# Gate matrix in DRAM: from blocks of sixteen columns per store to blocks of eight rows per load

## The chip, the cores and the metric

One core of a Trainium2 chip runs the whole program. The metric is the device time of one execution in microseconds, lower is better.

## The reference, cut to what matters

Two passes of one trunk layer (a context of 128 tokens and 1,024 latent tokens, nine tiles of 128 tokens in all) end in the PEER channel mixer. For every token, eight heads each choose 16 of 16,384 experts; the expert rows are dotted with the token, passed through gelu, weighted, and used to sum rows of a second table:

```
s = jnp.einsum('thpd,hpkd->thpk', q, keys)
v1, i1 = lax.top_k(s[:, :, 0], PEER_TOPK)
v2, i2 = lax.top_k(s[:, :, 1], PEER_TOPK)
...
act = jax.nn.gelu(jnp.einsum('tkd,td->tk', u_tab[ii], xi))
return jnp.einsum('tk,tkd->td', gi * act, v_tab[ii])
```

All data are float32.

## The kernel before, in words

The kernel has two ways for this mixer. Five of the nine tiles (GATHER) fetch the 128 chosen rows of each token by indirect DMA: GpSimd issues one gather per row of picks (`gather`, L1711), a ring of eight buffers of 512 KB takes them, and VectorE works them off, first the dots with rows of u (`dot`, L2257), then the weighted sum of rows of v (`add_row`, L2264). The other four tiles (DENSE, 512 tokens) go through all 16,384 experts in 128 chunks of 128: TensorE (PE) turns a block of u (L1957), multiplies it with the tokens (L1970), ACT applies gelu (L2184), GpSimd multiplies with the gate matrix (`weigh`, L1723), PE multiplies with a block of v (`values`, L1984), and VectorE adds the product (`add_dense`, L2341). The gate matrix has the weight of each expert for each of the 512 tokens, mostly zeros: 32 MB, kept in DRAM as tensor `g`.

The last function, `tail`, has two stages. The mixing stage runs 144 units, in three groups of three tiles: merge units (24 a group), out units (8) and query units (16). Each engine goes through the units in the same order, and work of other kinds is written into fixed slots of that order: picks of the top 16 (`pick_slot`), the first gathered rows (`dots_in`), and the making of the gate matrix, 128 batches of four tokens (`batches`), from unit 66 on. In a batch VectorE and ACT make two one-hot factors (L2328, L2071, L2076), PE multiplies them (`gates`, L1930), and ACT copies the product to a buffer (`gate_rows`, L2089). Four batches make 16 tokens, and ACT then waits for its own copy and stores them, 1 MB (L2092). There are two such buffers (`gbuf`), and ACT waits for the store of two blocks earlier before it fills one again (L2087). A block of `g` is [128 partitions, 128 chunks x 16 tokens], so a partition's 8 KB go out in one piece.

SyncE (SP) loads everything else of this stage, in unit order: for each unit it waits until PE is done, then loads the weights five units ahead (`load_unit`: a merge unit has 1,536 runs of 512 bytes, a query unit 1,024), then the stores of normed rows (`store_norm`) and of h2t (L1599, runs of 512 bytes), then the score rows for VectorE's picks (`load_head`, L1556). ACT also stores the score rows of the heads (`score_rows`, L2047) into two buffers in turn. After the last unit SP waits for all stores, the gates among them (L1637), and then starts the loads of the dense part: blocks of u (`load_u`, L1615), of v (`load_v`, L1621) and of gates (`load_g`, L1627). A gate load brings eight chunks for 16 of the 32 blocks, 1 MB: it picks 8 x 16 floats from each block and partition, 2,048 runs of 512 bytes. There are 32 loads, two for each eight chunks, into two buffers. GpSimd's `weigh` stands at fixed places among its gathers, and VectorE's `add_dense` at fixed places among its rows, so that 8.5 gathered rows go with one chunk.

```
part = slice(16 * b, 16 * b + 16)
sp.dma_start(gp[:, o % 2, part].rearrange("p b c t -> p b (c t)"),
             T["g"][part, :, OCT * o * BLK:OCT * (o + 1) * BLK].rearrange("b p n -> p b n"))
...
if (n + 1) % (BLK // HB) == 0:
    act.wait_ge(g_out, n + 1)
    act.dma_start(T["g"][q], gbuf[q % 2].rearrange("p c t -> p (c t)"))
```

Of the kernel before, what the change touches and what calls it, by code (L numbers as in the profile page):

```python
# [26 lines left out]
P = 128  # L27
# [3 lines left out]
TILES = 1 + LAT  # L31
# [6 lines left out]
PH, TOPK = 8, 16  # L38
# [1265 lines left out]
GROUPS = ((0, 1, 2), (3, 4, 5), (6, 7, 8))  # L1304
# [53 lines left out]
def tail(nc, T, keep):  # L1358
# [8 lines left out]
    units = weight_units()  # L1367
    NU = len(units)
# [5 lines left out]
    GC, OCT, BLK, HB = 4, 8, 16, 4  # L1374
    NB = P // HB
    NBATCH = ND * NB
# [17 lines left out]
    batches, n = {}, 0  # L1394
# [22 lines left out]
    pick_rows = {ROWS * (gi - 1) + 8 + 26 * j: (gi, j) for gi in range(2, len(GATHER)) for j in range(PH)}  # L1417
    number_of = lambda gi, j: (ND + gi) * PH + j if gi else j

    def place(s):  # L1420
        return GROUPS[units[s][1]]

    with nc.cleanup_on_exit(), ExitStack() as ctx:
        sb = lambda n, s, d=F32: ctx.enter_context(nc.sbuf_tensor(n, s, d))
# [15 lines left out]
        sc = route_or_g[:, 6 * D + 4 * GN:6 * D + 4 * GN + 2 * 2 * P].rearrange("p (s n) -> p s n", s=2)  # L1440
# [4 lines left out]
        gbuf = [late[:, (8 + 2 * b) * D:(10 + 2 * b) * D].rearrange("p (c t) -> p c t", c=P) for b in range(2)]  # L1445
# [8 lines left out]
        gp = route_or_g[:].rearrange("p (s b c t) -> p s b c t", s=2, b=32, c=OCT)  # L1454
# [43 lines left out]
        exd_in, exd_done, gwd_done, pk_t, pk_out, a_done, b_done, b_half, gm_done, g_out = (  # L1498
            sem(f"tl_{n}") for n in ("exd_in", "exd_done", "gwd_done", "pk_t", "pk_out", "a_done", "b_done", "b_half", "gm_done", "g_out"))
# [23 lines left out]
        def _(sp):  # L1523
# [26 lines left out]
            def load_head(number):  # L1550
                t, h = pick_tile[number], number % PH
                if number >= 4:
                    sp.wait_ge(picked, number - 3)
                o = score_of(t // GT, h, t % GT)
                sp.wait_ge(st_sc[o % 2], 16 * (o // 2) + 16)
                sp.dma_start(heads[:, number % 4].rearrange("p a n -> p (a n)"), T["sc"][t, h]).then_inc(head_in[number % 4], 16)  # L1556

            sp.dma_start(bm[:], T["b_merge"][0].rearrange("(c p) -> p c", p=P), allow_slow_non_contiguous=True).then_inc(bm_in, 16)
            sp.dma_start(gain2, T["g_norm2"].to_broadcast([P, D])).then_inc(gain_in, 16)
            sp.dma_start(keep.iota[:], T["const_iota"]).then_inc(iota_in, 16)  # L1560
            for t in range(GT):
                load_x(t)
            last_merge = {units.index(("merge", g, NM - 1)) + i: (g + 1, i) for g in range(NG - 1) for i in range(GT)}
            for d in range(NU):
                wait_unit(d)
                if d + W < NU:
                    load_unit(sp, T, keep, d + W, units[d + W])
                kind, g, j = units[d]
                if d < NM and d % 4 == 3 and d // 4 + 2 < NLATE:
                    a = d // 4 + 2  # L1570
                    sp.dma_start(keep.qat[a % 2], T["qat"][GT + a]).then_inc(keep.q_in[a % 2], 16)
                if d >= 5 and d % 4 == 1 and (d - 5) // 4 < NLATE:
                    a = (d - 5) // 4
                    sp.wait_ge(fy_out, a + 1)
                    sp.dma_start(T["yt"][GT + a][:, MIX:], keep.yat).then_inc(st_ya, 16)
                if d in last_merge:
                    to, i = last_merge[d]
                    load_states(sp, T, keep, to, i)
                    sp.wait_ge(st_ya, 16 * GT * to)
                    load_mixed(sp, T, keep, to, i)  # L1580
                if kind == "out" and g == 0 and j == NO - 1:
                    sp.wait_ge(y_read, 2)
                    load_row(sp, T, 1, gate1, 2, rows2_in)
                    sp.wait_ge(h2_done, 1)
                    load_row(sp, T, 1, scale2, 4, rows3_in)
                    load_row(sp, T, 1, shift2, 3, rows3_in)
                if kind == "merge" and g > 0 and j == 0:
                    store_norm(GT * (g - 1))
                    store_norm(GT * (g - 1) + 1)
                if kind == "merge" and g > 0 and j == 2:  # L1590
                    store_norm(GT * (g - 1) + 2)
                if kind == "out" and g == NG - 1 and j == NO - 1:
                    for i in range(GT):
                        store_norm(GT * g + i)
                if kind == "query" and j == 0:
                    for i, t in enumerate(GROUPS[g]):
                        if t in DENSE:
                            sp.wait_ge(h_out, 2 * t + 2)
                            sp.dma_start(T["h2t"][t].rearrange("p (k n) -> p k n", k=DC), merged[:, 0:DC, i * P:(i + 1) * P]).then_inc(st_h2t, 16)  # L1599
                for number, slot in enumerate(pick_slot):  # L1600
                    if slot == d + 2:
                        load_head(number)
                if d == 66:
                    sp.wait_ge(st_h2[0], 16)
                    sp.dma_start(h2g[:], T["h2"][GATHER[0]]).then_inc(h2g_in, 16)
                if kind == "query" and g == NG - 1 and j == 4:
                    sp.wait_ge(st_h2t, 16 * ND)
                    for i, t in enumerate(DENSE):
                        sp.dma_start(h2t[:, :, i * P:(i + 1) * P], T["h2t"][t].rearrange("p (k n) -> p k n", k=DC)).then_inc(h2t_in, 16)
                    for s in range(2):  # L1610
                        sp.dma_start(ut_in[:, s, :], T["peer_u"][0, s * P:(s + 1) * P, :]).then_inc(u_in[s], 16)
# [11 lines left out]
            def load_g(o, b):  # L1623
                if o >= 2:
                    sp.wait_ge(w_done, OCT * (o - 1))
                part = slice(16 * b, 16 * b + 16)
                sp.dma_start(gp[:, o % 2, part].rearrange("p b c t -> p b (c t)"),  # L1627
                             T["g"][part, :, OCT * o * BLK:OCT * (o + 1) * BLK].rearrange("b p n -> p b n")).then_inc(gp_in[o % 2], 16)

            for k in range(2):  # L1630
                sp.wait_ge(st_sc[k], 16 * TILES * PH // 2)
            for b in range(GT):
# [370 lines left out]
        def _(act):  # L2003
# [76 lines left out]
            def gate_rows(n):  # L2080

                q = n // (BLK // HB)
                act.wait_ge(gm_done, n + 1)
                if n == 0:
                    act.wait_ge(st_ya, 16 * NLATE)
                if n % (BLK // HB) == 0 and q >= 2:
                    act.wait_ge(g_stored[q % 2], 16 * (q // 2))  # L2087
                at = (n % (BLK // HB)) * HB
                nc.scalar.copy(gbuf[q % 2][:, :, at:at + HB], ps[:, 6 + n % 2, :].rearrange("p (t c) -> p c t", t=HB)).then_inc(g_out, 1)  # L2089
                if (n + 1) % (BLK // HB) == 0:  # L2090
                    act.wait_ge(g_out, n + 1)
                    act.dma_start(T["g"][q], gbuf[q % 2].rearrange("p c t -> p (c t)")).then_inc(g_stored[q % 2], 16)  # L2092

            def at_exp(u):
                act.wait_ge(ftop_done, u + 1)
# [23 lines left out]
            for s in range(NU + 2):  # L2119
# [20 lines left out]
                if s < NU:  # L2140
                    kind, g, j = units[s]
# [51 lines left out]
        def _(dve):  # L2193
# [250 lines left out]
SCRATCH = {"mod": [2, 6 * D], "ht": [TILES, P, D], "kv": [TILES, P, 2 * MIX], "og": [TILES, P, MIX],  # L2444
           "qat": [TILES, AD, AH * P], "qkt": [TILES, P, 2 * MIX], "yct": [TILES, P, MIX],
           "yt": [TILES, P, 2 * MIX], "h2t": [TILES, P, D], "x1": [TILES, P, D], "h2": [TILES, P, D],
           "sc": [TILES, PH, P, 2 * P], "g": [32, P, 16 * P]}


class Keep:  # L2450
# [84 lines left out]
```

## Time and profile before

| | |
|---|---|
| median of 3 runs | 4637.36 us (4629.52 to 4639.0) |
| the profiled execution, its own time | 4641.09 us |
| its span | 4639.4 us |
| mean granted TensorE clock | 0.926 |
| PE busy | 4069.0 us (88%) |
| VectorE busy | 3055.6 us (66%) |
| GpSimd busy | 1853.7 us (40%) |
| ACT busy | 1065.6 us (23%) |
| DMA | 1134.98 MB, mean 245 GB/s |

The shares are averages over the whole span; the first 1,400 us are projections, the mLSTM and attention, where the change has no part. The mixing stage with gates runs from about 1640 to 2446 us, the dense part from there to the end. A DMA share of 1.00 means that all 16 DMA engines had a packet in hand all the time.

### The profile page before, as it was taken

The numbers are of one execution on the slowest core, as the hardware profiler recorded it, in microseconds if no ns is written. First come the engines' busy times: TensorE is split into PE (matmuls) and PEld (weight loads), VectorE is DVE, ScalarE is ACT, GpSimd is POOL, SyncE is SP. The second block draws the span as 40 slices with busy tenths as digits, with TensorE's granted clock in tenths as the row PEclk, the third lists the DMA queues.
The fourth block names the chain that finished last, engine by engine and source line by source line (L and its number), as shares of the span: only waits on it lengthen the run. The fifth ranks groups of instructions, "written<-read, shape, count | busy, mean of one in ns | idle before, by whom it ended". The sixth has DMA issues, their size and how long they took to land.

```text
span 4639.4 us, 42665 instructions
## 1 busy us (share of the span) xinstructions
PE 4069.0 (88%) x13326; PEld 2216.4 (48%) x13326; DVE 3055.6 (66%) x6574; ACT 1065.6 (23%) x2384; POOL 1853.7 (40%) x1519
## 2 busy tenths in 40 slices
PE   7799995889999988789885998989889988999993
PEld 1455555666655555556452443444434443444441
DVE  0111114843334986688566888999889988998798
ACT  0111111334411155567571110111101100111110
POOL 0000000000000024115015777777777777678784
PEclk9899996869999999899897999999989998999996
DMA  7311102622246359558459999999999999999996
GB/s 275 146 51 50 51 35 63 201 78 71 69 129 203 109 194 349 180 177 320 144 188 357 371 343 338 352 373 352 342 349 353 369 341 329 359 374 393 381 383 245
DMA packets 557069, 1134.98 MB, mean 245 GB/s; under 512 B 44348, under 2 KB 305980, under 8 KB 551744
## 3 DMA queue, kind: packets, MB, share of 16 engines
q0 software_dynamic: 187312, 680.61, 38.9%
q1 hardware_dynamic: 354584, 408.99, 26.6%
q10 hardware_dynamic: 14976, 43.00, 2.4%
q8 instruction: 94, 1.54, 0.1%
q14 instruction: 103, 0.84, 0.1%
HBM read 1048.12 MB, written 84.33 MB: 244 GB/s over the span
## 4 chain that ended last, share of the span: by engine, by line
PE 22%; DVE 22%; POOL 13%; DMA 9%; issue 9%; ACT 2%; SPq 1%; DVEq 0%; ACTq 0%; POOLq 0%
POOL late L1711 11%; DVE tl_acc L2264 6%; DMA late<-in_peer_u,ids 5%; PE tl_ps L1809 4%; PE tl_ps L1879 4%; DVE late L2257 4%; PE tl_ps L1984 3%; PE tl_ps L1970 2%; PE tl_ps L1852 2%; PE tl_ps L1827 2%; PE tl_ps L1930 2%; DMA late<-in_peer_v,ids 1%; DMA s_sc<-tl_route_or_g 1%; POOL big L1723 1%; DMA big<-in_peer_u 1%
## 5 line engine op out<-in xcount | busy, mean ns | idle before, releaser
L1711 POOL DMA_INDIRECT late<-in_peer_u,ids x640 | 851.0, 1330 | 871.6 <-DVE late L2257 650.2
L1984 PE MATMUL tl_ps<-big 128*128 128x512 f32 x2048 | 947.0, 617 | 149.8 <-POOL big L1723 145.3
L1711 POOL DMA_INDIRECT late<-in_peer_v,ids x640 | 758.1, 1185 | 422.0 <-DVE tl_acc L2264 251.9
L2264 DVE SCALAR_TENSOR_TENSOR tl_acc<-late,big,tl_acc 128x1024 f32<-128x1024 f32 x640 | 862.1, 1347 | 96.9 <-DMA late<-in_peer_v,ids 43.0
L2257 DVE SCALAR_TENSOR_TENSOR late<-late,tl_h2g 128x1024 f32<-128x1024 f32 x640 | 812.8, 1304 | 155.8 <-DMA late<-in_peer_u,ids 152.0
L1970 PE MATMUL tl_ps<-big 128*128 128x512 f32 x2048 | 904.1, 594 | 0.0
L1984 PEld LDWEIGHTS tl_ps<-big 128*128 128x128 f32 x2048 | 403.8, 199 | 676.7 <-issue 510.0
L1970 PEld LDWEIGHTS tl_ps<-big 128*128 128x128 f32 x2048 | 381.2, 191 | 431.5 <-issue 431.5
L1809 PE MATMUL tl_ps<-big 128*128 128x384 f32 x1152 | 398.5, 497 | 6.8 <-ACT tl_route_or_g L2045 4.5
L2163 ACT COPY big<-tl_ps 128x512 f32<-128x512 f32 x256 | 138.0, 589 | 1046.6 <-PE tl_ps L1957 1046.5
L378 PE MATMUL pj_ps_z<-big,late 128*128 128x512 f32 (+2 forms) x1008 | 365.4, 521 | 8.7 <-DMA big<-in_w_in 8.0
L1809 PEld LDWEIGHTS tl_ps<-big 128*128 128x128 f32 x1152 | 216.7, 194 | 156.4 <-issue 28.6
L378 PEld LDWEIGHTS pj_ps_z<-big,late 128*128 128x128 f32 x1008 | 183.0, 193 | 194.4 <-issue 178.4
L1879 PE MATMUL tl_ps<-big 128*128 128x384 f32 x768 | 267.7, 506 | 1.4 <-ACT big L2022 1.4
L2184 ACT ACTIVATE big<-tl_ps 128x512 f32<-128x512 f32 x128 | 76.5, 597 | 786.1 <-PE tl_ps L1970 786.1
L1930 PE MATMUL tl_ps<-tl_hot_or_fin 128*128 128x128 f32 x1024 | 151.3, 303 | 101.1 <-DVE tl_hot_or_fin L2328 55.5
L2076 ACT ACTIVATE tl_hot_or_fin<-tl_hot_or_fin,big 128x128 f32<-128x128 f32 x512 | 211.0, 482 | 4.3
L1827 PE MATMUL tl_ps<-big 128*128 128x384 f32 x576 | 200.9, 492 | 8.1 <-DVE big L2205 4.7
L1930 PEld LDWEIGHTS tl_ps<-tl_hot_or_fin 128*128 128x128 f32 x1024 | 140.0, 213 | 134.9 <-DVE tl_hot_or_fin L2328 72.6
L1879 PEld LDWEIGHTS tl_ps<-big 128*128 128x128 f32 x768 | 150.2, 200 | 100.3 <-issue 12.4
L1693 POOL TENSOR_TENSOR tl_ss<-tl_ss,tl_half 128x1 f32<-128x1 f32 x9 | 12.8, 1441 | 442.3 <-DVE tl_ss L2235 442.3
L1957 PE MATMUL tl_ps<-ident,big 128*128 128x128 f32 x1024 | 137.6, 279 | 55.3 <-DMA big<-in_peer_u 55.2
(309 smaller groups left out, 4111.5 us busy)
## 6 DMA issues: line engine op xcount, KB each, us to landing
big<-in_peer_u SPq DMA_DIRECT2D x128, 512.0 KB, 7.2
big<-in_peer_v SPq DMA_DIRECT2D x128, 512.0 KB, 9.2
big<-in_w_merge SPq DMA_DIRECT2D x72, 512.0 KB, 3.9
s_g<-late ACTq DMA_DIRECT2D x32, 1024.0 KB, 6.2
tl_route_or_g<-s_g SPq DMA_DIRECT2D x32, 1024.0 KB, 22.1
late<-in_w_ada SPq DMA_DIRECT2D x12, 2048.0 KB, 7.9
big<-in_w_peer_q SPq DMA_DIRECT2D x48, 512.0 KB, 5.2
big<-in_w_branch SPq DMA_DIRECT2D x72, 256.0 KB, 4.3
```

Source lines behind the costliest of these rows:

```text
L378: mm = nc.tensor.matmul(ps_z[j % 3][:, 0:n], ht[:, k, :], weights(k, c0, n), start=(k == 0), stop=(k == DC - 1))
L1711: nc.gpsimd.indirect_dma_start(ring[:, n % R, :], None, table[0], bass.IndirectOffsetOnAxis(ap=keep.ids[:, at:at + 1], axis=0)).then_inc(r ...
L1809: mm = nc.tensor.matmul(ps[:, j % 2, 0:GN].rearrange("p (i n) -> p i n", i=GT), wring[:, s % W, k * P:(k + 1) * P], states[:, :, k, :], st ...
L1827: mm = nc.tensor.matmul(ps[:, 2 + j % 2, 0:GN].rearrange("p (i n) -> p i n", i=GT), wring[:, s % W, D + k * P:D + (k + 1) * P], states[:, ...
L1879: mm = nc.tensor.matmul(ps[:, 4 + j % 2, 0:GN], wring[:, s % W, k * P:(k + 1) * P], merged[:, k, :], start=(k == 0), stop=(k == DC - 1))
L1930: mm = nc.tensor.matmul(ps[:, 6 + n % 2, u * P:(u + 1) * P], hot[:, n % 2, 1, u, :], hot[:, n % 2, 0, u, :], start=True, stop=True)
L1970: mm = nc.tensor.matmul(ps_a[s % 2], utt[:, s % 2, k, :], h2t[:, k, :], start=(k == 0), stop=(k == DC - 1))
L1984: mm = nc.tensor.matmul(ps_o[v % 2][:, b, :], w[:, slot, i * P:(i + 1) * P], vch[:, slot, b * 512:(b + 1) * 512], start=(c == 0), stop=(c ...
L2076: a = nc.scalar.activation(hot[:, n % 2, 1, u, :], hot[:, n % 2, 1, u, :], ACT.Relu, bias=pickt[i % 2][:, 2, t:t + 1], scale=minus[i % 2][ ...
L2163: nc.scalar.copy(dst, src).then_inc(t_out, 1)
L2257: nc.vector.scalar_tensor_tensor(out=ring[:, n % R, :], in0=ring[:, n % R, :], scalar=1.0, in1=h2g[:], op0=ALU.mult, op1=ALU.mult, accum_o ...
L2264: nc.vector.scalar_tensor_tensor(out=acc[:], in0=ring[:, n % R, :], scalar=wts[:, k:k + 1], in1=acc[:], op0=ALU.mult, op1=ALU.add).then_in ...
```

## The change

The tensor `g` becomes [16 sets of eight chunks, 128 partitions, 32 blocks of 16 tokens, 128 floats]. A gate load then finds the 16 blocks of a partition next to each other, 8 KB in one piece, and a store scatters a partition's 8 KB over 16 places, 512 bytes each. The stores are issued by SP: block q when SP has come to the unit in which ACT handles batch 4q + 5 (units 68 to 142), behind that unit's weight loads, norm stores and score rows, the last two blocks after all units. ACT's wait for its own copy and its DMA instruction go. The unused function `place` goes too.

```diff
-    def place(s):
-        return GROUPS[units[s][1]]
+    slot_of = {n: s for s, some in batches.items() for n in some}
+    PER = BLK // HB
+    gate_store_at = {}
+    for q in range(NBATCH // PER):
+        gate_store_at.setdefault(min(slot_of.get(PER * q + PER + 1, NU), NU), []).append(q)
...
+            def store_gates(q):
+                sp.wait_ge(g_out, PER * q + PER)
+                sp.dma_start(T["g"][:, :, q, :].rearrange("o p n -> p o n"),
+                             gbuf[q % 2].rearrange("p (o c) t -> p o (c t)", c=OCT)).then_inc(g_stored[q % 2], 16)
...
                     if slot == d + 2:
                         load_head(number)
+                for q in gate_store_at.get(d, []):
+                    store_gates(q)
...
                 part = slice(16 * b, 16 * b + 16)
-                sp.dma_start(gp[:, o % 2, part].rearrange("p b c t -> p b (c t)"),
-                             T["g"][part, :, OCT * o * BLK:OCT * (o + 1) * BLK].rearrange("b p n -> p b n")).then_inc(gp_in[o % 2], 16)
+                sp.dma_start(gp[:, o % 2, part].rearrange("p b c t -> p b (c t)"), T["g"][o, :, part, :]).then_inc(gp_in[o % 2], 16)
+
+            for q in gate_store_at.get(NU, []):
+                store_gates(q)
             for k in range(2):
                 sp.wait_ge(st_sc[k], 16 * TILES * PH // 2)
...
-                if (n + 1) % (BLK // HB) == 0:
-                    act.wait_ge(g_out, n + 1)
-                    act.dma_start(T["g"][q], gbuf[q % 2].rearrange("p c t -> p (c t)")).then_inc(g_stored[q % 2], 16)
...
-           "sc": [TILES, PH, P, 2 * P], "g": [32, P, 16 * P]}
+           "sc": [TILES, PH, P, 2 * P], "g": [16, P, 32, P]}
```

## Rows read from the trace of the kernel before

**Rows 1.** Windows: stretch, us, busy (count) per engine, PEclk, DMA share, GB/s.
```profile
1800.00:1850.00 50.00, 42.51 (x184) 29.49 (x183) 28.22 (x48) 34.34 (x91) 26.36 (x21) 0.90 1.04 393
...
1840.00:1860.00 20.00, 11.74 (x44) 8.52 (x44) 5.60 (x36) 10.67 (x29) 0.00 (x0) 0.76 0.93 298
...
2540.00:4190.00 1650.00, 1510.68 (x4009) 705.86 (x4008) 1461.64 (x2467) 176.75 (x313) 1219.89 (x972) 0.95 0.95 351
4190.00:4560.00 370.00, 361.99 (x968) 168.47 (x966) 314.93 (x362) 37.58 (x68) 297.61 (x241) 1.00 1.01 386
```

**Rows 2.** The gate tensor's transfers by line, then the page's DMA issues (median landing).
```profile
L2092 ACTq DMA_DIRECT2D s_g<-late x32: 326/326/357, 1659.7 to 2437.9; - x32
L1627 SPq DMA_DIRECT2D tl_route_or_g<-s_g x32: 378/434/13606, 2446.7 to 4355.1; - x32
...
s_g<-late ACTq DMA_DIRECT2D x32, 1024.0 KB, 6.2
tl_route_or_g<-s_g SPq DMA_DIRECT2D x32, 1024.0 KB, 22.1
```

**Rows 3.** DMA queues (packets, MB, share) in 4420:4480, then 2620:2680, then 2000:2100.
```profile
q1 hardware_dynamic: 1089, 3.95, 16.9%
...
DMA packets 9257, 22.83 MB, mean 380 GB/s; under 512 B 687, under 2 KB 4118, under 8 KB 9255
...
q1 hardware_dynamic: 4615, 5.95, 28.6%
...
q10 hardware_dynamic: 576, 4.19, 10.1%
```

**Rows 4.** Chain in order of time (start, us, what) at the hand-over.
```profile
2437.94 8.21 DMA s_g<-late
...
2447.21 13.61 SPq L1627
```

**Rows 5.** Timeline at the start of the dense part: GpSimd's first weighting, then PE.
```profile
2483.27 1.26 POOL L1723 TENSOR_TENSOR big<-big,tl_route_or_g 128x512 f32<-128x512 f32 x1 [11.38 <-DMA tl_route_or_g<-s_g]
...
2487.09 1.97 PE L1957 MATMUL tl_ps<-ident,big 128*128 128x128 f32 x8 [24.36 <-DMA big<-in_peer_u]
...
2529.02 1.97 PE L1957 MATMUL tl_ps<-ident,big 128*128 128x128 f32 x8 [8.32 <-DMA big<-in_peer_u]
...
2539.65 5.74 PE L1984 MATMUL tl_ps<-big 128*128 128x512 f32 x13
```

**Rows 6.** Waits, 2530:4560 (PE) and 2500:2700 (VectorE); timeline's first, last row wait.
```profile
PE tl_ps L1984 <- POOL big L1723: 145.3, 24, 13.9
...
DVE late L2341 <- PE tl_ps L1984: 28.7, 8, 15.7
...
2706.24 2.92 DVE L2257 SCALAR_TENSOR_TENSOR late<-late,tl_h2g 128x1024 f32<-128x1024 f32 x1 [0.34 <-DMA late<-in_peer_u,ids]
...
4189.31 1.25 DVE L2257 SCALAR_TENSOR_TENSOR late<-late,tl_h2g 128x1024 f32<-128x1024 f32 x1 [1.11 <-DMA late<-in_peer_u,ids]
```

**Rows 7.** Chain in order of time in the mixing stage.
```profile
1843.81 4.69 SPq L1336
1848.59 5.27 DMA tl_heads<-s_sc
...
2310.04 6.10 DMA s_sc<-tl_route_or_g
```

**Rows 8.** Timeline of SP and ACT in the mixing stage.
```profile
1811.32 16.39 SPq L1599 DMA_DIRECT2D s_h2t<-big  x2
...
2309.19 8.93 SPq L1336 DMA_DIRECT2D big<-in_w_peer_q  x2
...
2316.22 0.37 ACT L2045 COPY tl_route_or_g<-tl_ps 128x256 f32<-128x256 f32 x1 [5.38 <-DMA s_sc<-tl_route_or_g]
...
2380.90 1.28 ACT L2071 ACTIVATE tl_hot_or_fin<-iota,big 128x128 f32<-128x128 f32 x4 [0.46 <-ACT late L2089]
...
2401.84 0.37 ACT L2045 COPY tl_route_or_g<-tl_ps 128x256 f32<-128x256 f32 x1 [1.00 <-DMA s_sc<-tl_route_or_g]
```

## The prediction

> **What bounds the kernel now.** I read the windows by stage first, to see where DMA, SyncE (SP) and the compute engines are short of room, then the DMA queues for the price of a run, then the chain and the timeline where the mixing stage hands over to the dense part, and last the waits inside each stage. The gate matrix is written from 1659.7 to 2446 us, while the mixing stage runs, and its loads are issued from 2446.7 to 4355.1 us, in the dense part [rows 2]. In the dense part DMA is busy 95% to 101% of the time, and TensorE (PE) 92% of 2540 to 4190 and 98% of 4190 to 4560 [rows 1]. So a cheaper load looks like a direct gain. Two things speak against reading it so. Inside 2540 to 4190, PE's only real wait is for GpSimd's weighting, 145.3 us in 24 waits, and that is paced by the gathered rows that VectorE works off [rows 6]. And VectorE's waits for gathered rows do not follow the gate loads: between 2700 and 4190 there are 96 of them, 96.1 us in all, the first at 2706.24 and the last at 4189.31 [rows 6]. Sorted by whether a gate load was issued in the 24 us before, 36.0 us fall into 528 us with a load and 60.1 us into 962 us without: 0.068 and 0.063 us of wait per us. The gate loads are hidden there; what decides is the hand-over at 2446 us and the mixing stage, which gets the short runs.
>
> **The price of a run.** A stretch without a gate load gives SP's queue 1,089 packets and 3.95 MB in 16.9% of 16 engines for 60 us: 162 us for about 964 packets of 4 KB, 168 ns each. In the next stretch the same queue moves 5.95 MB in 28.6%, 275 us; some 3,431 packets are of 512 bytes (4,118 less 687), the remaining 4.19 MB are 1,024 packets of 4 KB or 172 us, so a 512-byte packet takes about 30 ns. ACT's queue writes 4.19 MB in 10.1% of 100 us, 512 packets of 8 KB at 316 ns [rows 3]. A gate transfer of 1 MB is thus 2,048 x 30 = 61 us of engine time in short runs, 3.8 us on 16 engines, and 128 x 316 = 40 us, 2.5 us, in long ones. The change moves 1.3 us of full DMA time per transfer, 32 times, from the dense part to the mixing stage: 42 us at most each way.
>
> By the Trainium skill (DMA: Bandwidth & Descriptors, Specifications) a transfer runs at line rate from 512 bytes on; then nothing would be moved, the dense term below would be zero and the total 4642 us. The rows disagree: 17 GB/s per engine at 512 bytes, 24 at 4 KB.
>
> **The dense part's loads.** Of the 32 loads, 24 are issued in 2540 to 4190: 24 x 1.3 = 31 us of DMA time. By the sorted waits above almost none of it is waited for; I take a sixth, **-5 us** (bounds 0 and -31). From 4190 on PE is full, so 0.
>
> **The hand-over.** Now ACT's last store takes 8.21 us to land, SP then issues a block of u and two gate loads, and the second gate load holds SP 13.61 us [rows 4]. GpSimd waits 11.38 us for the gate blocks until 2483.27, PE waits 24.36 us for one block of u and, two blocks later, 8.32 us, and the first values matmul starts at 2539.65 [rows 5]. The two gate loads and one u block are 264 packets per engine and take from 2446.8 to 2483.2, 138 ns a packet, because a gathered 4 KB packet (168 ns) gets in between most of them. After the change:
> - The last store leaves SP as 128 short packets per engine, behind gathers: 128 x 138 ns = 17.7 us instead of 8.2, **+10 us** before SP starts (bounds +0 and +18). The cover of the old store was its size: 8 packets per engine.
> - The two gate loads are then 16 packets of 8 KB, each beside one gathered packet: 16 x (316 + 168) = 7.7 us instead of some 35. The third u block, behind them, two v blocks and one earlier u, each 8 x 336 ns = 2.7 us, lands about 2477 instead of 2487. The next one has nine more 0.5 MB transfers in front, 27 us: about 2504; the next, behind one gate load, about 2511 instead of 2529. From there to the first values PE needs 10.6 us, and a little more as it has the block before still to do: 2524 instead of 2539.65. I take **-14 us** with the later start included (bounds +8 and -33, the latter if all of the 24.36 and 8.32 went).
> It reaches the end, because VectorE waits 28.7 us for PE's values in 2500 to 2700, 15.7 of it at the first [rows 6]. What is late next is the gathered row: those transfers now take a larger share from the gathers.
>
> **The mixing stage.** Each of the 32 stores moves from ACT's queue to SP's, behind one wait per store for the copies (g_out). Queued behind that wait are SP's weight loads, prefetched five units ahead, its norm stores and the loads of score rows for VectorE's picks. The wait itself costs nothing, as ACT has made the copy by the time SP's unit is done; if ACT were late, the score rows would be late first.
> - ACT is freed of a wait on its own copy: 0.46 us idle behind the store [rows 8], 32 x 0.46 = 14.7 us; only in the query units is ACT on the chain, so a third: **-5 us** (0 and -15).
> - SP's queue is short of room at 1811 to 1849: two stores of h2t hold it 16.39 us [rows 8], query weights 4.69 us more at the end, and the chain runs from there through the score rows, 5.27 us, into VectorE's pick [rows 7]. Two gate stores (of units 82 and 85) now lie in front of those score rows: 2 x 3.8 = 7.7 us less the 2 x 2.5 that ACT's stores took from the same engines, and a little for order: **+6 us** (0 and 2 x 17.7 = +35).
> - ACT's third score store of a head waits for the first to land: 5.38 us where SP has just issued query weights (1,024 runs), 1.00 us where it has not [rows 8], and the first kind is on the chain with 6.10 us [rows 7]. So SP's 1,024 runs cost 4.4 us; 2,048 more may cost up to 8.8. In three units of the last group (131, 137, 139) a gate store goes out right before scores: 3 x 4 = **+12 us** (0 and +26).
> - The saturated stretches (DMA 1.04 at 1800 to 1850 [rows 1]) get 1.3 us more work per store, and the gate buffer is two deep: a store that takes 17.7 us instead of a median 6.2 [rows 2] can make ACT wait to refill it. Six such stores, a little each: **+6 us** (0 and +20).
>
> By the Trainium skill (DMA: Bandwidth & Descriptors, Latency and other measured facts) copies with row pitches of 512 KiB ran at 207 GB/s and of 2 MiB at 164. The new store's runs lie 2 MiB apart within a partition, and by that ratio each short packet would take 38 ns instead of 30; for the ten stores on the path that would add 10 us, 4646 in all. No row of this kernel writes with that pitch. I keep the 30 ns, of reads 1 MiB apart; either rule's total lies in the forecast's own range.
>
> **Sum.** -5 - 14 - 5 + 6 + 12 + 6 = 0 against the profiled execution (4641.09 us, span 4639.4). The median of the three runs stands 3.7 us lower, so **4637 us**. A measurement here can tell about 0.2% (9 us) from no change.
>
> **Rivals.**
> 1. **The dense part is bound by DMA after all.** For it: the share of 0.95 to 1.01, and waits for gathered rows [rows 1, 6]. Then the 31 us come off in full instead of 5, and the hand-over gains 25 rather than 14: 4637 - 26 - 11 = 4600 us. Against: the sorted waits.
> 2. **SP's queue at 1811 to 1849 decides, slower.** If a gate store holds SP for the 17.7 us that gathers beside it make, rather than 3.8, the score rows come 35 us late instead of 6 and the pick, then PE, with them: 4637 + 29 = 4666 us. It decides once a store holds the queue above about 10 us each. For: a 2,048-run load held SP 13.61 us [rows 4]. Against: GpSimd issues no gather from 1840 to 1860 [rows 1], so the queue drains alone by then.
> 3. **The change doesn't do what it says**: the loads stay 2,048 packets, because the runs on the chip's side are cut. Then only the costs of the mixing stage and the later start remain: 4637 + 5 + 24 = 4666 us. Against: source and target are both 8 KB in one piece per partition.
>
> **Chances.** The forecast (gain at the hand-over, given back in the mixing stage) 0.50, with its own range 4617 to 4657; rival 1 0.25, rival 2 0.22, rival 3 0.03. Of the forecast's 0.50 I put 0.16 faster by over 0.2%, 0.24 within, 0.10 slower; of rival 1, 0.24 faster and 0.01 within; of rivals 2 and 3, 0.23 slower and 0.02 within. So faster 0.40, same 0.27, slower 0.33. Range: from a little beyond rival 1 (4595) to rival 2 (4668).
>
> **What would show it.** The gate load's median to landing falls from 22.1 to under 10 us and the store's rises above 6.2; GpSimd's 11.38 us wait is gone and the first values matmul comes 15 us earlier after the last gate copy; 0.46 us gaps behind ACT's stores vanish. Right in the dense part: PE's waits for the weighting stay near 145 us; under 120 makes rival 1 right. Score rows that land more than 15 us later after 1811 make rival 2 right. Wrong altogether: a mixing stage that does not get longer, or PE waiting there for weights.

## The result, and the profile after

The changed kernel took 4657.43 us (median of 20 runs, 4646.34 to 4677.69), the kernel before in the same comparison 4636.32 us (20 runs, 4624.93 to 4655.4). The ratio is 1.0047, 95% interval [1.0036, 1.0058]: 21 us slower, inside the predicted range, but not the "no change" that was forecast.

The profiled execution of the changed kernel has a span of 4661.3 us, 21.9 more than before. First, from the page, ScalarE's DMA queue (packets, MB, share), which now has the score rows alone, and the DMA issues (median landing), to be set beside [rows 2]; then the trace's answer for the line of the gate stores (landing: shortest, median, longest).

```profile
q10 hardware_dynamic: 10368, 9.44, 0.6%
...
s_g<-late SPq DMA_DIRECT2D x32, 1024.0 KB, 7.5
tl_route_or_g<-s_g SPq DMA_DIRECT2D x32, 1024.0 KB, 10.3
```

```profile
L1566 SPq DMA_DIRECT2D s_g<-late x32: 359/439/2680, 1671.2 to 2465.5; - x32
...
DMA to landing us min/median/max: 5.0/7.5/36.0
```

The loads do what the change says: 10.3 us to landing instead of 22.1 (under 10 was forecast). The stores look harmless by their median, 7.5 instead of 6.2 us. Their longest tells more: 36.0 us, where the kernel before had 10.0 (the landing line for L2092, whose first line stands in [rows 2]):

```profile
DMA to landing us min/median/max: 3.9/6.2/10.0
```

ScalarE's waits of the mixing stage (1640 to 2480) have a group that the kernel before did not have, and two rows of its timeline carry most of it (36.5 of the 57.0 us). L2100 is the copy of a gate product into the buffer (L2089 before), L1566 SyncE's store.

```profile
ACT late L2100 <- PE tl_ps L1941: 111.1, 39, 11.2
ACT tl_route_or_g L2056 <- DMA s_sc<-tl_route_or_g: 65.3, 19, 6.7
ACT late L2100 <- DMA s_g<-late: 57.0, 5, 18.3
```

```profile
1711.00 0.57 ACT L2100 COPY late<-tl_ps 128x512 f32<-128x512 f32 x1
...
1756.06 0.59 ACT L2100 COPY late<-tl_ps 128x512 f32<-128x512 f32 x1 [18.35 <-DMA s_g<-late]
...
1801.92 0.56 ACT L2100 COPY late<-tl_ps 128x512 f32<-128x512 f32 x1
...
1845.53 0.59 ACT L2100 COPY late<-tl_ps 128x512 f32<-128x512 f32 x1 [18.14 <-DMA s_g<-late]
```

The chain of work that ended last passes, of all 32 stores, through just these two, of blocks 2 and 5:

```profile
1720.00 35.98 DMA s_g<-late
...
1817.61 27.84 DMA s_g<-late
```

Read the four copies with the two stores. Block 2's last copy ends at 1711.57; its store is issued at 1720.00, 8.4 us later, and lands 36.0 us after that, so the buffer is free 44.4 us after the copy. For block 5 it is 15.1 and 27.8, 42.9 us in all. The kernel before shows how long the buffer could be done without: from the end of a block's last copy to the first copy two blocks on, with no wait for a store in between.

```profile
1705.13 0.57 ACT L2089 COPY late<-tl_ps 128x512 f32<-128x512 f32 x1
...
1740.18 0.59 ACT L2089 COPY late<-tl_ps 128x512 f32<-128x512 f32 x1 [4.12 <-PE tl_ps L1930]
...
1792.99 0.56 ACT L2089 COPY late<-tl_ps 128x512 f32<-128x512 f32 x1
...
1818.93 0.56 ACT L2089 COPY late<-tl_ps 128x512 f32<-128x512 f32 x1
```

That is 34.5 us for block 2 and 25.4 for block 5. The changed stores overrun by 9.9 and 17.5, 27.4 us together. Set against the kernel before, the copies are 5.9 us late in the first batches (5.6 at the very first one, before any store: a difference of the two executions), 2.2 late at batch 15, 26.6 late at batch 28, which had to wait for block 5, and 27.6 late at the last copy: the mixing stage lost 21.7 us.

At the hand-over SyncE starts the dense part's first load at 2484.61, 19.1 us after the last copy instead of 8.4, since it now waits for the last store:

```profile
SPq L1648 <- DMA s_g<-late: 18.4, 1, 18.4
```

```profile
2484.61 0.34 SPq L1625 DMA_DIRECT2D big<-in_peer_u  x1
2485.00 0.90 SPq L1637 DMA_DIRECT2D tl_route_or_g<-s_g  x2
```

```profile
2551.37 7.13 PE L1995 MATMUL tl_ps<-big 128*128 128x512 f32 x16
```

The last of these lines is PE's first values matmul. Two gate loads no longer hold SyncE (0.90 us for two, where one held it 13.61 [rows 4]), and the first values matmul comes 85.9 us after the last copy instead of 101.7 [rows 5]: 15.8 gained. By the Gelu values of chunk 16 the gain is still 15.8 us; at the last chunk it is 5.7. So the span's 21.9 us are 5.9 + 21.7 - 15.8 + 10.1, the last being what the dense part loses of the gain again.

### The profile page after: what moved, and what is told of

Same layout as the page of the kernel before. It is cut to its first block, busy times and chain, and to the rows that moved or that the text cites. A ratio compares the mean times of both kernels' runs of the same rounds, so it can differ in the third digit from the quotient of the medians.

```text
span 4661.3 us, 42665 instructions
## 1 busy us (share of the span) xinstructions
PE 4075.5 (87%) x13326; PEld 2220.7 (48%) x13326; DVE 3060.5 (66%) x6574; ACT 1061.7 (23%) x2384; POOL 1853.3 (40%) x1519
## 3 DMA queue, kind: packets, MB, share of 16 engines
q10 hardware_dynamic: 10368, 9.44, 0.6%
## 4 chain that ended last, share of the span: by engine, by line
DVE 23%; PE 20%; DMA 12%; POOL 11%; issue 9%; ACT 2%; DVEq 0%; ACTq 0%; SPq 0%; POOLq 0%
POOL late L1722 10%; DVE tl_acc L2272 7%; DMA late<-in_peer_u,ids 6%; DVE late L2265 4%; PE tl_ps L1820 4%; PE tl_ps L1890 4%; DMA late<-in_peer_v,ids 3%; PE tl_ps L1863 2%; PE tl_ps L1995 2%; PE tl_ps L1838 2%; PE tl_ps L1941 2%; DMA s_sc<-tl_route_or_g 2%; PE tl_ps L1981 1%; DMA s_g<-late 1%; POOL big L1734 1%
## 5 line engine op out<-in xcount | busy, mean ns | idle before, releaser
L1995 PE MATMUL tl_ps<-big 128*128 128x512 f32 x2048 | 946.6, 617 | 161.6 <-POOL big L1734 158.5
L2272 DVE SCALAR_TENSOR_TENSOR tl_acc<-late,big,tl_acc 128x1024 f32<-128x1024 f32 x640 | 872.5, 1363 | 105.9 <-DMA late<-in_peer_v,ids 51.5
L1704 POOL TENSOR_TENSOR tl_ss<-tl_ss,tl_half 128x1 f32<-128x1 f32 x9 | 12.8, 1441 | 448.4 <-DVE tl_ss L2243 448.4
L1968 PEld LDWEIGHTS tl_ps<-ident,big 128*128 128x128 f32 x1024 | 122.3, 143 | 105.8 <-issue 65.3
## 6 DMA issues: line engine op xcount, KB each, us to landing
tl_route_or_g<-s_g SPq DMA_DIRECT2D x32, 1024.0 KB, 10.3
```

The costliest lines, as they stand in the source:

```text
L1995: mm = nc.tensor.matmul(ps_o[v % 2][:, b, :], w[:, slot, i * P:(i + 1) * P], vch[:, slot, b * 512:(b + 1) * 512], start=(c == 0), stop=(c ...
L2272: nc.vector.scalar_tensor_tensor(out=acc[:], in0=ring[:, n % R, :], scalar=wts[:, k:k + 1], in1=acc[:], op0=ALU.mult, op1=ALU.add).then_in ...
```

## The experiments

My theory after the traces: ScalarE's waits to refill the two-deep buffer make the loss, because stores are issued late and land late; the loads give back some of it at the hand-over. Times below are medians; each ratio is to the kernel before on the same chip in the same comparison (12 runs of a kernel or fewer, 23 to 30 of the kernel before).

### Loads alone, stores alone

```diff
# a_long_loads: the kernel before, and
-  T["g"][part, :, OCT * o * BLK:OCT * (o + 1) * BLK].rearrange("b p n -> p b n")
+  T["g"].rearrange("b p n -> (b p n)").rearrange("(o p b n) -> o p b n", o=16, p=P, b=32)[o, :, part, :]
# b_sp_short_only: the changed kernel, and
-  T["g"][o, :, part, :]
+  T["g"].rearrange("o p b n -> (o p b n)").rearrange("(b p n) -> b p n", b=32, p=P)[part, :, OCT * o * BLK:OCT * (o + 1) * BLK].rearrange("b p n -> p b n")
```

> The kernel before, its stores untouched (ScalarE, 8 KB runs), but the dense part's loads read the same bytes as if they lay in the new order, so in 8 KB runs; the gate values that it multiplies with are therefore those of other rows, which changes no duration. This is the loads' side of the change alone. My theory (the mixing stage pays, the loads give back some): copies of the gates as before, last copy within 3 us of the kernel before, the first Gelu values of the dense part 14 to 20 us earlier, of which the dense part hands back about 10, so 4 to 14 us faster, ratio 0.997 to 0.999. Rival (the loads cost too, through the gathers): within 3 us of before or slower.

> The changed kernel's stores (SyncE, 512-byte runs) with the old loads in 512-byte runs, which read the same bytes as if they lay in the old order (gate values of other rows). The stores' side alone. My theory: gate copies late as in the changed kernel, by 18 to 25 us at the last one, and nothing gained at the hand-over: 22 to 40 us slower than before, ratio 1.005 to 1.0085. Rival (the loads cost): less than 15 us slower.

Measured: loads alone 4627.1 us beside 4633.51, ratio 0.9992 [0.9974, 1.0009]; stores alone 4666.34 us, 1.0069 [1.0044, 1.0094]. The two add up to 1.0061, near the change's 1.0047 [1.0036, 1.0058]. The loss is the stores'. The loads' side is some 4 to 6 us, which its interval does not tell from nothing; it lies between the theory's 0.997 to 0.999 and the rival's "within 3 us".

It also settles the first rival, whose 37 us (4637 to 4600) the interval excludes. Waits of VectorE for gathered rows, 2560 to 4140, before and then with long loads:

```profile
DVE late L2257 <- DMA late<-in_peer_u,ids: 81.9, 81, 4.0
...
DVE tl_acc L2264 <- DMA late<-in_peer_v,ids: 7.5, 12, 2.3
```

```profile
DVE late L2257 <- DMA late<-in_peer_u,ids: 87.3, 67, 4.5
...
DVE tl_acc L2264 <- DMA late<-in_peer_v,ids: 14.6, 14, 2.8
```

The loads land in 10.5 us instead of 22.1, and VectorE waits 101.9 us for rows instead of 89.4. The lighter loads did not bring the rows sooner, so the DMA share of 0.95 is no sign that 31 us were to be had in the dense part.

### Shape or issuer

```diff
# c_act_short: the changed kernel, SyncE's store_gates calls taken out, and behind ScalarE's copy
+  if (n + 1) % (BLK // HB) == 0:
+      act.wait_ge(g_out, n + 1)
+      act.dma_start(T["g"][:, :, q, :].rearrange("o p n -> p o n"), gbuf[q % 2].rearrange("p (o c) t -> p o (c t)", c=OCT)).then_inc(g_stored[q % 2], 16)
# d_sp_long: the changed kernel with the old tensor, the old loads, and in store_gates
+  sp.dma_start(T["g"][q], gbuf[q % 2].rearrange("p c t -> p (c t)")).then_inc(g_stored[q % 2], 16)
```

> The changed kernel, but each store is issued by ScalarE right behind its copies, as before, in 512-byte runs on ScalarE's own queue. It parts the shape of the store from its issuer. Theory shape (512-byte packets beside gathers land late whoever issues them): longest store still over 25 us, ScalarE's wait to refill the buffer 30 us or more in all, and the time 10 to 22 us over before, ratio 1.002 to 1.005. Theory issuer (the store is late because it stands in SyncE's queue behind weights, norm rows and score rows): longest store under 15 us, refill wait under 10 us, and the time 4 to 14 us under before.

> The kernel before, layout and 8 KB runs kept, but the stores are issued by SyncE at the changed kernel's places. Theory shape: longest store under 15 us, refill wait under 10 us, time within 5 us of before. Theory issuer: stores of 25 us and more, refill wait of 30 us or more, time 15 to 30 us over before (the gate loads stay in 512-byte runs, so nothing is gained at the hand-over).

> The run with all stores on ScalarE in 512-byte runs, again, for a closer interval: 4627 beside 4633.5 the first time, 0.9995 [0.998, 1.001]. Theory (the gain of the hand-over stays, the stores cost nothing at the end): 3 to 12 us under before, upper end of the interval at or below 1.0005. Rival: no difference, within 3 us of before.

Measured: short runs issued by ScalarE 4627.02 us, 0.9995 [0.998, 1.001], and again 4635.74 beside 4629.83, 1.0006 [0.9991, 1.0022]: no difference, so the second expectation was missed and the small gain of the first run did not repeat. Long runs issued by SyncE 4632.27 us, 1.0002 [0.9987, 1.0017]. Neither theory was right alone. Each half makes ScalarE wait about 25 us for its buffer (14.2 in the second run with short runs), and neither half costs time that these intervals show:

```profile
ACT late L2096 <- DMA s_g<-late: 27.3, 4, 10.2
```

```profile
ACT late L2099 <- DMA s_g<-late: 23.6, 4, 9.2
```

Block 2's store, by the answers for the lines of the stores (first short runs by ScalarE, then long runs by SyncE), stays within the 34.5 us both times: 34.3, and 8.4 from copy to issue and 18.6 to landing.

```profile
L2099 ACTq DMA_DIRECT2D s_g<-late x1: 366/366/366, 1707.9 to 1707.9; - x1
...
DMA to landing us min/median/max: 34.3/34.3/34.3
```

```profile
L1566 SPq DMA_DIRECT2D s_g<-late x1: 430/430/430, 1718.9 to 1718.9; - x1
...
DMA to landing us min/median/max: 18.6/18.6/18.6
```

### The same stores, issued earlier by SyncE

```diff
             for d in range(NU):
+                for q in gate_store_at.get(d, []):
+                    store_gates(q)
                 wait_unit(d)
...
-                for q in gate_store_at.get(d, []):
-                    store_gates(q)
```

> The changed kernel, with SyncE's store of a gate block moved ahead of everything else in its unit (ahead of the wait for the unit's weights, the next weights, norm rows and score rows) instead of behind it. Blocks 2 and 5, whose landing ScalarE waited for with 18.4 and 18.1 us in the changed kernel, were issued 8.4 and 15.1 us after their last copy there. My theory (the cost is late issue plus slow landing, each of which alone fits into the slack): issue within 1 us of the copy, ScalarE's refill wait from 57 to 20 to 35 us, the last copy 12 to 22 us earlier against the kernel before than in the changed kernel, time 4 to 14 us under before to 5 over, ratio 0.997 to 1.001. Rival (short runs behind the weights in one queue land late wherever they are issued): refill wait 45 us or more, time 15 to 25 us over before.

Measured: 4634.99 us beside 4636.3, 1.0004 [0.9988, 1.002]; the loss is gone, as the theory has it (the queue was the same, SyncE's). Refill waits fell from 57.0 to 28.4 us, the last copy came 17.1 us earlier. Block 2 was issued 2.7 us after its copy (within 1 was expected) and landed in 32.0. Block 5, issued at once instead of 15.1 us late, landed in 6.2 us instead of 27.8: the later slot had put it into a busier moment. While it landed here, the gathers moved 77 packets; in the changed kernel, while it landed, 2,656.

```profile
L1566 SPq DMA_DIRECT2D s_g<-late x1: 377/377/377, 1797.2 to 1797.2; - x1
...
DMA to landing us min/median/max: 6.2/6.2/6.2
```

### Two stores of 32

```diff
# l_two_on_act: the changed kernel with ON_ACT = (2, 5); m_two_on_sp: all but (2, 5)
         for q in range(NBATCH // PER):
+            if q in ON_ACT:
+                continue
             gate_store_at...
...
+                if (n + 1) % PER == 0 and q in ON_ACT:
+                    act.wait_ge(g_out, n + 1)
+                    act.dma_start(...)
```

> The changed kernel, but of its 32 stores the two of blocks 2 and 5 are issued by ScalarE right behind the copies (512-byte runs still). Theory (the loss of the mixing stage hangs on these two stores, issued 8 and 15 us late and then 36 and 28 us in landing; the waits at blocks 20 to 22 took the place of waits for TensorE): the refill wait at blocks 4 and 7 falls from 36.5 us to under 12, the last copy comes 12 to 24 us earlier against the kernel before than in the changed kernel, time 12 to 24 us under the changed kernel, ratio to before 0.9995 to 1.0025. Rival (all waits count alike): a third to a half of the loss stays, ratio 1.003 or more.

> The converse: the run with all stores on ScalarE (512-byte runs, 8 KB loads), except that blocks 2 and 5 are stored by SyncE at the changed kernel's places. Theory: these two alone bring back 15 to 24 us of the last copy, and the time rises by as much over that run: 4640 to 4652, ratio to before 1.001 to 1.004. Rival (the loss is spread over the 32 stores): within 6 us of the run with all stores on ScalarE, ratio under 1.0005.

Measured: with these two on ScalarE and the other 30 on SyncE 4623.93 us beside 4629.83, 0.9988 [0.9973, 1.0002], some 27 us under the changed kernel by the ratios, a little more than expected. With these two on SyncE and the other 30 on ScalarE 4656.85 us, 1.0057 [1.004, 1.0074], above the expected 1.004, and 21.1 us over the second run with all stores on ScalarE, where 15 to 24 were expected. The whole loss of the mixing stage sits in two stores. ScalarE's refill waits, first of the faster kernel, then of the slower, with the latter's chain:

```profile
ACT late L2103 <- DMA s_g<-late: 33.1, 4, 10.4
```

```profile
ACT late L2103 <- DMA s_g<-late: 64.8, 5, 25.0
```

```profile
1721.20 39.30 DMA s_g<-late
...
1827.39 29.82 DMA s_g<-late
```

33.1 us of waits at blocks 8 and 20 to 22 cost nothing that shows; about 45 us at blocks 4 and 7 cost 21 to 27. The measure that fits is the overrun of the slack of 34.5 and 25.4 us. From copy's end to landing, blocks 2 and 5, the overrun, and how much later batch 28's copy came against batch 15's than before:

| kernel | block 2 | block 5 | overrun | lateness | ratio |
|---|---|---|---|---|---|
| changed | 8.4 + 36.0 | 15.1 + 27.8 | 27.4 | 24.4 | 1.0047 |
| stores alone | 8.4 + 36.7 | 17.5 + 27.0 | 29.7 | 24.8 | 1.0069 |
| two on SyncE | 8.4 + 39.3 | 20.6 + 29.8 | 38.2 | 34.2 | 1.0057 |
| long runs by SyncE | 8.4 + 18.6 | 19.7 + 10.6 | 4.9 | 7.4 | 1.0002 |
| issued earlier | 2.7 + 32.0 | 0 + 6.2 | 0.2 | 5.7 | 1.0004 |
| short runs by ScalarE | 0 + 34.3 | 0 + 6.2 | 0 | -1.5 | 0.9995, 1.0006 |
| two on ScalarE | 0 + 31.1 | 0 + 6.5 | 0 | -1.3 | 0.9988 |
| ring of six (next section) | 8.5 + 36.4 | 17.1 + 20.5 | 22.6 | 10.0 | 1.0314 |

The last row does not fit: an overrun of 22.6 us, and a lateness of 10.0 that is gone again at the last copy (0.1). The slack was read from the kernel before, with its ring of eight; in the kernel with the shorter ring ScalarE waited only 12.0 and 12.8 us for these two stores.

### A third buffer

The room for a third buffer, 8 KB per partition, came from the ring of gathered rows, and the shorter ring has a run of its own.

```diff
# f_ring6
-    R = 8
+    R = 6
# g_three_bufs: and three buffers from late[6 * D:12 * D], q % 3 for q % 2 in buffers, semaphores and waits
```

> The changed kernel with a ring of 6 gathered rows instead of 8: the control of the next run, since the room for a third gate buffer has to come from the ring. Refill wait 45 to 65 us as in the changed kernel; the shorter ring may cost something in the dense part, 0 to 60 us.

> The ring of 6 with a third gate buffer in the room of the two rows. Theory (ScalarE's wait to refill the two-deep buffer is what the mixing stage pays): the refill wait falls under 5 us, the last gate copy comes 15 to 28 us earlier than in the run with two buffers, and the time falls by 15 to 28 us against it. Rival (the mixing stage pays for SyncE's queue, weights and score rows, whatever the buffer): under 8 us between the two.

Measured: ring of six 4774.17 us beside 4636.3, 1.0314 [1.0295, 1.0333]; with the third buffer 4766.41, 1.029 [1.0273, 1.0307]. The refill wait went from 24.9 us to none, the last copy came 10.2 us earlier and the time fell by 7.8. The copies speak for the theory, but the time is under the 15 to 28 us it expected and just on the rival's side of the line, so these two runs alone don't decide. With six rows in flight the waits were only 24.9 us to start with (45 to 65 were expected), so there was less to win. The ring's own price, 2.7%, was twice what I had allowed.

### Two versions meant to be faster

```diff
# i_act_short_order: short runs by ScalarE, and at the start of the dense part
+            sp.wait_ge(s_done, TILES * PH)
+            load_u(2)
+            load_v(0)
+            load_v(1)
             for b in range(2):
                 sp.wait_ge(g_stored[b], 16 * ND * P // BLK // 2)
-            sp.wait_ge(s_done, TILES * PH)
-            load_u(2)
             load_g(0, 0)
             load_g(0, 1)
-            load_v(0)
-            load_v(1)
             load_u(3)
# h_first_set: the kernel before, and
+  act.dma_start(T["g0"][:, q, :], gbuf[q % 2][:, 0:OCT, :].rearrange("p c t -> p (c t)")).then_inc(g_stored[q % 2], 16)
+  act.dma_start(T["g"][q][:, OCT * BLK:], gbuf[q % 2][:, OCT:, :].rearrange("p c t -> p (c t)")).then_inc(g_stored[q % 2], 16)
...
+  load_g reads T["g0"][:, part, :] where o == 0; "g0": [P, 32, 8 * 16]; g_stored counts 32 per block
```

> A version meant to beat both: stores by ScalarE in 512-byte runs, loads in 8 KB runs, and SyncE issues the dense part's next block of peer_u and the first two of peer_v ahead of its wait for the last gate store (the gate loads stay behind it). In the run with ScalarE's stores SyncE began these loads 22 us after the last copy. Theory (the row stream is what the dense part runs at, and VectorE sets its pace): first Gelu values up to 15 us earlier than there, but the end only 0 to 6 us earlier: 4620 to 4628 beside 4633 of before, ratio 0.997 to 0.999. Rival (the hand-over is worth its full size at the end): 12 us or more under the run with ScalarE's stores.

> The kernel before, with the gates of the first eight rows (the first two gate loads' set) kept a second way: ScalarE stores each block as one 512-byte run per partition into a small tensor of its own and the other 7.5 KB as before; the first two loads read 8 KB runs, the other 30 still 512-byte runs. Theory (VectorE's row work sets the dense part's pace, so only what the hand-over gains counts): as good as long loads throughout, mixing as before, 3 to 12 us under before, ratio 0.9975 to 0.9995. Rival (the 512-byte loads of the later sets cost in the dense part as well): within 3 us of before.

Measured: the new order 4637.37 us beside 4636.3, 1.0008 [0.9996, 1.0019]. It missed: after the last copy its Gelu values were 20 us ahead of before at chunk 4 (13 with the old order), 11 at chunk 6, 5 at the end. Bringing u and v forward did not carry through.

The first set kept twice: 4622.7 us beside 4629.83, 0.9986 [0.9974, 0.9998]. It is the only version whose interval lies below 1, by 6 to 7 us (0.14%), less than the 0.2% that I called measurable ahead of the result. ScalarE has no refill wait in it, and the long stores still land fast, while 30 of 32 loads keep their 512-byte runs:

```profile
L2093 ACTq DMA_DIRECT2D s_g<-late x32: 327/450/670, 1667.8 to 2445.0; - x32
...
DMA to landing us min/median/max: 3.8/5.7/10.7
```

As far as these intervals tell, the two first loads are worth about as much as all 32; a direct comparison of the two was not made.

## Why the prediction was wrong, and where it was right

**The step that failed** is the last term of the mixing stage: "the gate buffer is two deep: a store that takes 17.7 us instead of a median 6.2 [rows 2] can make ACT wait to refill it. Six such stores, a little each: **+6 us** (0 and +20)". The mechanism was named and under-sized, beyond its own bound. What it cost is about 27 us, give or take 8 (changed kernel against the run with two stores on ScalarE, by the ratios), and it was two stores, not six. Three things went into the miss.

- The 17.7 us came from the hand-over's 138 ns a packet. Block 2's store of short runs took 31 to 39 us, whoever issued it.
- The sentence "The wait itself costs nothing, as ACT has made the copy by the time SP's unit is done" looked only at who stands behind the store. It left out how long the store stands behind SyncE's own work: 8.4 us for block 2 (the loads of two units, and 3.9 us of waiting for TensorE between them) and 15.1 for block 5 (query loads, then 8.2 us of waiting for a store of the residual rows to land). To that came a landing of 27.8 us instead of 6.2 at the later moment.
- No slack was read. The timeline before had it, 34.5 and 25.4 us. Against these a landing of 17.7 us makes no wait if the store is issued at once; 15.1 + 17.7 would have overrun by 7.4, and 8.4 + 36.0 overran by 9.9.

The other terms together came out as forecast, and that is luck. The forecast has -5 - 14 - 5 + 6 + 12 = -6 us for them; the run with two stores on ScalarE, which is the changed kernel without these two late stores, measured -5.6 us (interval -12.5 to +1). But its mixing stage did not get longer (last copy 2.4 us earlier than before), so the +6 and +12 were not there, and about 6 of the -24 came. In the same way the mixing stage's 21.7 us in the trace look like the forecast's sum of +19 for it, and are made of another term.

**The hand-over** was right up to the first values matmul: -14 forecast, -15.8 measured, with the parts as written (SyncE's start 10.7 us later for a predicted 10; GpSimd's 11.38 us wait for gates gone; the first values matmul 15.8 us earlier after the last copy for a predicted 15). The step behind it, "It reaches the end, because VectorE waits 28.7 us for PE's values", held only in part. The wait for values went, and waits for gathered rows took the place of some of it: from 92 us after the last copy on, for 2,030 us, 36.3 us fell to 8.8, and 141.5 rose to 153.0. First before (2530 to 4560), then after (2557.6 to 4587.6):

```profile
DVE late L2257 <- DMA late<-in_peer_u,ids: 125.1, 133, 4.4
DVE late L2341 <- PE tl_ps L1984: 36.3, 14, 15.7
DVE tl_acc L2264 <- DMA late<-in_peer_v,ids: 16.4, 21, 2.3
```

```profile
DVE late L2265 <- DMA late<-in_peer_u,ids: 129.3, 113, 4.0
DVE tl_acc L2272 <- DMA late<-in_peer_v,ids: 23.7, 27, 3.5
DVE late L2349 <- PE tl_ps L1995: 8.8, 9, 2.4
```

The chain at the hand-over shows the change of hands: before it goes through u blocks to PE (44.21 us), after through three gathered rows.

```profile
2484.76 44.21 DMA big<-in_peer_u x2
```

```profile
2486.39 16.01 DMA late<-in_peer_v,ids
...
2505.03 17.86 DMA late<-in_peer_v,ids
...
2524.47 19.09 DMA late<-in_peer_v,ids
```

How much is left at the end is not settled. In this execution it is 5.7 us; from the last copy to the end, the eight profiled executions with long loads and a ring of eight are 1.3 to 19.5 us shorter than the one execution before (mean 11.7), the two with short loads 2.7 and 3.1. Two of the eight are of one kernel (short runs by ScalarE) and differ widely, 17.1 and 1.3. The times say less: loads alone gained about 4 us, with an interval of -12 to +4 that leaves out the -14, and more so the -19 of hand-over and loads together.

**The dense part's loads**, -5 forecast: nothing that can be told from zero, and the argument for it held. The waits of TensorE for the weighting stayed (145.3 [rows 6], 158.5 after), so the first rival is out, by the run with long loads alone too, which was 6 us faster where the rival wanted 31 from the loads inside the dense part.

**The price of a run**, 30 ns, was right. In the run with ScalarE's short stores its queue holds 76,416 packets in 3.1% of 16 x 4622.4 us, 2,293 us; less the score rows' 0.6% of 16 x 4661.3 us in the changed kernel (447 us, 10,368 packets) that is 1,846 us for 66,048 packets, 28 ns.

```profile
q10 hardware_dynamic: 76416, 43.00, 3.1%
```

The pitch rule of the Trainium skill (DMA: Bandwidth & Descriptors, Latency and other measured facts) that the prediction weighed gave 38 by its ratio (and 4647 in all, not 4646). It is measured for the pitch from partition to partition, and this store's 2 MiB lie between the runs of one partition; the 28 ns show no such loss here.

**The other terms of the mixing stage.** Score rows at 1811 to 1849, +6: not there; VectorE's wait for them is 4.3 us after and 19.2 before. Held score stores, +12: ScalarE's waits for them rose from 59.5 to 65.3 us, but from batch 90 to the last copy the lateness fell from 29.8 to 27.6, so none of it shows on the path. ScalarE's own-copy wait, -5: the wait (13.3 us in 29 before) is gone; its worth at the end was not measured apart.

**The second rival** had the time (4666) and one of the two places, 1811 to 1849, and another mechanism: not score rows behind a store, but the store behind SyncE's norm rows. Its sign came all the same: the first score rows after 1811 landed 11.8 us later than before, the next 28.6. But with 30 of the stores still on SyncE and only blocks 2 and 5 on ScalarE, both landed 3.3 and 6.2 us later, in an execution that had begun 4.9 late; the delay was ScalarE's wait, handed on. The third is out by the loads' landing.

## What to carry to other kernels

When a transfer that frees a buffer is moved, reshaped or given to another issuer, read its deadline first: from the last write into the buffer to the first write that reuses it, block by block. Compare that with the time until the new issuer gets to it plus its landing in the busiest stretch, not with the median landing; the cost is the overrun of the few blocks with the least slack. Two half measures that each fit, or nearly fit, into the slack can overrun it together.

## What the runs showed of the hardware that was not expected

A store of 1 MB in 512-byte runs takes its engines only about 1.4 times as long as in 8 KB runs (129 packets per engine at 28 ns against 9 packets, (2.4% - 0.6%) of 16 x 4639.4 us over 4,608 packets, 290 ns), and where the engines are free it lands nearly as fast: 5.0 us at the least against 3.9. Beside gathers and weights the gap is 34.3 to 7.0 us for the same block from the same queue. The Trainium skill (DMA: Bandwidth & Descriptors, Queues, rings and completion order) says that each engine goes round the queues and takes one packet from each in turn, and puts some 9 to 17 descriptors into a packet. The trace agrees on the turns and not on the size: each run of 512 bytes takes a turn of its own. While block 2's store of the changed kernel landed (1720 to 1756 us), the gathers' queue and SyncE's moved the same number of packets, but the gathers three times the bytes:

```profile
q0 software_dynamic: 3026, 11.02, 75.6%
q1 hardware_dynamic: 3030, 3.62, 27.9%
```

With ScalarE as issuer a third queue takes turns: 2,095 packets of the gathers and 2,107 of SyncE went by in the 34.3 us, beside the store's own 2,064. Per engine that is 34.3 us for 129 packets, 0.27 us each, some nine times its own 28 ns. Block 5's store, issued at once in the same run, has the engines nearly to itself (1793.2 to 1799.4 us, no packet of SyncE's queue), and lands in 6.2 us:

```profile
q10 hardware_dynamic: 2064, 1.05, 65.0%
q0 software_dynamic: 80, 0.33, 18.9%
```

The Trainium skill's figure for line rate from 512 bytes on (DMA: Bandwidth & Descriptors, Specifications), which the prediction weighed, says nothing of this.

The Trainium skill (DMA: Bandwidth & Descriptors, Issuing engines are not separate DMA queues) holds that another issuer saves only the time on the sequencer that it takes to initiate the DMA, "usually small relative to the DMA itself". The initiation is small here too, a median 439 ns on SyncE. What counted is another time, which that sentence does not speak of: 8.4 to 20.6 us until SyncE, with other work before it in its program, came to the store.

A ring of six gathered rows instead of eight cost 2.7%. The rows landed sooner (median 7.0 us instead of 8.0), yet VectorE's waits for them in 2560 to 4140 rose from 106.8 us in the changed kernel to 208.5:

```profile
DVE late L2265 <- DMA late<-in_peer_u,ids: 138.8, 108, 4.9
...
DVE tl_acc L2272 <- DMA late<-in_peer_v,ids: 69.7, 69, 3.5
```

What sets the pace of the gathered rows in the dense part, and so how much of an earlier start lasts to the end, was not tried further.
